# Up projection of a GeGLU block in seven half products for each pair of tiles, with the down projection behind it

## What is computed

```python
def conv_ffn(h, w_up, conv_w, conv_b, w_down, conv_state):
    u = jnp.einsum('btd,df->btf', h, w_up)             # 1024 -> 2 * 2816
    a, b = u[..., :D_FF], u[..., D_FF:]
    a_ext = jnp.concatenate([conv_state.astype(a.dtype), a], axis=1)
    conv = conv_b
    for j in range(CONV_W):                            # causal, width 3
        conv = conv + conv_w[j] * a_ext[:, j:j + T]
    out = jnp.einsum('btf,fd->btd', jax.nn.gelu(conv, approximate=True) * b, w_down)
```

## Time and profile before

| | us |
|---|---|
| median of 3 runs | 1754.72 |
| lowest and highest run | 1752.34, 1755.62 |
| span of the profiled execution (no other time of it is given) | 1750.5 |
| PE busy in that span | 1720.8 |

### The profile page before, as it was taken

How to read it: one execution, slowest core, us unless ns; L and a number is a source line. 1 busy time by engine, 2 the same in 40 slices (tenths; PEclk the granted TensorE clock), 3 DMA queues, 4 the chain that set the end, 5 groups by cost and what they waited for, 6 DMA issues and landing times.

```text
span 1750.5 us, 27949 instructions
## 1 busy us (share of the span) xinstructions
PE 1720.8 (98%) x11791; PEld 1640.1 (94%) x11791; DVE 749.9 (43%) x1027; ACT 494.6 (28%) x816; POOL 160.3 (9%) x232
## 2 busy tenths in 40 slices
PE   7999999999999999999999999999999999999998
PEld 6999889888888899999978999999999999999997
DVE  6421244444530255565544453433424434434345
ACT  5211244434443244331233321121121211211212
POOL 5100000000010024300033300000000000000001
PEclk9999999999999999999999999999999999999999
DMA  9774433231247686343441211102111111021004
GB/s 358 233 224 152 151 103 117 89 126 54 90 144 227 158 251 157 88 145 133 162 140 67 94 49 49 49 25 65 48 34 49 49 49 49 25 72 47 27 13 192
DMA packets 161038, 190.33 MB, mean 109 GB/s; under 512 B 14306, under 2 KB 139506, under 8 KB 160921
## 3 DMA queue, kind: packets, MB, share of 16 engines
q1 hardware_dynamic: 140488, 171.17, 30.3%
q10 hardware_dynamic: 19424, 17.21, 3.1%
q0 software_dynamic: 1008, 0.23, 0.1%
HBM read 146.70 MB, written 41.87 MB: 108 GB/s over the span
## 4 chain that ended last, share of the span: by engine, by line
PE 68%; ACT 1%; DVE 1%; issue 1%; POOL 0%; DVEq 0%; ACTq 0%; POOLq 0%
PE ps L162 46%; PE ps L1455 10%; PE ps L2655 4%; PE ps L2730 1%; PE ps L3230 1%; PE ps L3201 1%; PE ps L1811 0%; PE ps L2264 0%; PE ps L2222 0%; PE ps L2256 0%; PE ps L2625 0%; PE ps L2712 0%; POOL h_a L2441 0%; PE ps L2258 0%; PE ps L1821 0%
## 5 line engine op out<-in xcount | busy, mean ns | idle before, releaser
L162 PE MATMUL ps<-mg_hi,w_hi 128*128 128x352 f32 x1008 | 218.0, 324 | 0.3 <-issue 0.3
L162 PE MATMUL ps<-mg_hi,w_lo 128*128 128x352 f32 x1008 | 217.3, 323 | 0.0
L162 PE MATMUL ps<-mg_lo,w_hi 128*128 128x352 f32 x1008 | 217.0, 323 | 0.0
L162 PEld LDWEIGHTS ps<-mg_hi,w_lo 128*128 128x128 f32 x1008 | 173.1, 188 | 0.0
L162 PEld LDWEIGHTS ps<-mg_hi,w_hi 128*128 128x128 f32 x1008 | 171.6, 189 | 0.5 <-issue 0.5
L162 PEld LDWEIGHTS ps<-mg_lo,w_hi 128*128 128x128 f32 x1008 | 171.2, 188 | 0.0
L3056 DVE TENSOR_TENSOR f_t<-f_t,ps 128x1056 f32<-128x1056 f32 x80 | 100.3, 1253 | 151.2 <-PE ps L162 151.2
L147 DVE TENSOR_TENSOR w_lo<-w_raw,w_hi 128x2048 fp32r<-128x2048 f32 x59 | 136.7, 2317 | 56.8 <-ACT w_hi L143 56.8
L143 ACT ACTIVATE w_hi<-w_raw 128x2048 fp32r<-128x2048 f32 x59 | 112.9, 1914 | 124.6 <-PE ps L162 120.0
L1332 PE MATMUL ps<-acts_hi,w_hi 128*128 128x352 f32 x384 | 132.8, 346 | 2.9 <-ACT out_z L1164 2.3
L1455 PE MATMUL ps<-acts_hi,w_hi 128*128 128x352 f32 x384 | 128.0, 333 | 3.9 <-PEq L1073 2.3
(11 more groups left out here) (452 smaller groups left out, 3034.7 us busy)
## 6 DMA issues: line engine op xcount, KB each, us to landing
w_raw<-in_w_up SPq DMA_DIRECT2D x22, 1024.0 KB, 5.1
w_raw<-in_w_in SPq DMA_DIRECT2D x21, 1024.0 KB, 5.8
w_ada_chunks<-in_w_ada ACTq DMA_DIRECT2D x32, 512.0 KB, 7.4
w_raw<-in_w_down SPq DMA_DIRECT2D x11, 1024.0 KB, 4.8
z_scratch<-out_z SPq DMA_DIRECT2D x48, 176.0 KB, 1.8
z_scratch<-gate_ev SPq DMA_DIRECT2D x48, 176.0 KB, 4.7
w_ada_chunks<-in_w_ada SPq DMA_DIRECT2D x16, 512.0 KB, 8.3
chunks<-z_scratch SPq DMA_DIRECT2D x24, 256.0 KB, 4.4
```

Source lines behind the costliest of these rows:

```text
L162: mm = pe.matmul(ps[:, bank + b, 0:TB], w[wi][:, k, j * P:(j + 1) * P], (a_hi, a_lo)[ai][:, k, b * TB:(b + 1) * TB], start=(n == 0), stop= ...
```

## The change

**Units.** The up projection goes in units of one chunk (two output tiles), 22 in all; even units are a chunks, odd ones b chunks. Unit 0 stays an ordinary product (in four banks of 264 columns instead of three of 352). Units 1 to 21 take Strassen's scheme: the two output tiles, the two halves of the inner size (4 x 128 each) and the two halves of the tokens (528 each) form 2 x 2 blocks, and seven half products replace eight. A half product is 4 inner tiles x 3 passes x 2 banks = 24 matmuls of 264 columns.

**Sums in front.** Four sums of token blocks (T1 to T4, 128 x 2112 numbers each) are made once, between unit 0 and unit 1, by DVE and POOL, and split. For every unit POOL makes four sums of weight blocks (128 x 512), and all seven weight pieces of 512 columns are split by ACT and DVE one at a time, each as soon as its product of the unit before has ended.

**Sums behind.** The seven products accumulate in three pairs of banks; ACT copies intermediate sums out, DVE adds three of them from PSUM for each unit.

**Order.** The down projection no longer alternates with the up projection: all units come first. The rows g of ten pairs go to DRAM (`g_store`) and come back (`g_load`) for ten down pairs afterwards; the last pair stays on chip. The first down pair copies into `f_t`, so its clearing falls away. Token columns are reordered into four groups of 256 prompt tokens and 8 sample tokens, which splits some copies of the mixer in two.

```diff
+def half_product(u, r, bank, columns, first):
+    w = [piece(x, r) for x in (whi_all, wlo_all)]
+    order = products(HK)
+    pe.wait_ge(wp_lo, product(u, r))
+    for n, (k, wi, ai) in enumerate(order):
+        for q in range(2):
+            mm = pe.matmul(ps[:, bank + q, 0:QW], w[wi][:, k, :], columns(ai, k, q), ...)
+    mm.then_inc(u_prod, 1)
...
+def unit(u):                                   # on PE
+    half_product(u, A11, xb, of_h2(0, 0), True)
+    if u > 1: pe.wait_ge(y_added, ops_until(u - 1))
+    half_product(u, A12, YB, of_h2(HK, 0), True)
+    pe.wait_ge(x_copied, p1_copied(u))
+    if u == 1: pe.wait_ge(t_lo_s, 1)
+    half_product(u, PS2, xb, of_t(T2_), False)
+    ...                                        # u == 1: t_lo_s 2, else v_added
+    half_product(u, PS1, VB, of_t(T1_), True)
+    pe.wait_ge(x_copied, 2 * ops_until(u))     # u == 1: t_lo_s 3 too
+    half_product(u, PS3, xb, of_t(T3_), False)
+    pe.wait_ge(v_copied, ops_until(u))
+    half_product(u, PS4, VB, of_h2(HK, 2), False)
+    pe.wait_ge(x_added, ops_until(u))          # u == 1: t_lo_s 4 too
+    half_product(u, A22, xb, of_t(T4_), False)
...
+def weight_sums(u):                            # on POOL, for every unit
+    ...                                        # waits for the load, and from u = 3 for piece PS4 of unit u - 1
+    pool.tensor_tensor(at_(PS1), weight_part(u, PS1), weight_part(u, A22), ALU.add)
+    pool.tensor_tensor(at_(PS2), at_(PS1), weight_part(u, A11), ALU.subtract)
+    pool.tensor_tensor(at_(PS3), weight_part(u, A11), weight_part(u, PS1), ALU.subtract)
+    pool.tensor_tensor(at_(PS4), weight_part(u, A12), at_(PS2), ALU.subtract)
...
+pool.wait_ge(h_lo, NTT)                        # start of the part, POOL
+pool.tensor_tensor(r22[:], b22(mg_hi), b22(mg_lo), ALU.add)
+weight_sums(1)
+pool.tensor_tensor(t_raw[T3_][:], r22[:], r12[:], ALU.subtract)
...                                            # then clears, state copies, weight_sums(2)
+dve.wait_ge(h_lo, NTT)                         # start of the part, DVE
+dve.tensor_tensor(r12[:], b12(mg_hi), b12(mg_lo), ALU.add)
+dve.tensor_tensor(t_raw[T1_][:], r12[:], b11(mg_hi), ALU.subtract)
+dve.tensor_tensor(t_raw[T1_][:], t_raw[T1_][:], b11(mg_lo), ALU.subtract)
+dve.wait_ge(t_pool, 1)
+dve.tensor_tensor(t_raw[T2_][:], r22[:], t_raw[T1_][:], ALU.subtract)
+dve.tensor_tensor(t_raw[T4_][:], b21(mg_hi), t_raw[T2_][:], ALU.subtract)
+t_low(T2_, 2)
+piece_lo(dve, 1, PS2)
+t_low(T1_, 2)
+piece_lo(dve, 1, PS1)
+y_add(1)
+dve.tensor_tensor(t_raw[T4_][:], t_raw[T4_][:], b21(mg_lo), ALU.add)
+piece_lo(dve, 1, PS3)
+t_low(T3_, 3)
+piece_lo(dve, 1, PS4)
+piece_lo(dve, 1, A22)
+x_add(1)
+t_low(T4_, 4)
...                                            # pieces of unit 2, v_add(1), convolutions 0 and 1, b times g
+for u in range(2, UNITS_UP):                   # on DVE
+    piece_lo(A11 of u + 1); y_add(u); piece_lo(A12, PS2); x_add(u)
+    piece_lo(PS1, PS3); v_add(u); piece_lo(PS4)
+    # a units: convolve(u), piece_lo(A22), convolve(u + 1); b units: three products with g, piece_lo(A22)
...
-for k in range(KT):
-    pool.memset(f_t[:, k, :], 0.0).then_inc(f_add, 1)
...
+for i in range(DOWN_PAIRS):                    # on PE, behind the units and the 44 transposes
+    pe.wait_ge(w_lo_ready, FFN0 + 2 + i)
+    pe.wait_ge(g_lo_s, i + 1)
+    for k in range(KT):
+        ...                                    # k 0: y_added, v_added; k 1: lv_rows; else the add two tiles back
+        gemm_tile(pe, i % 2, 2, D_MODEL, k, g_hi[i % 2], g_lo[i % 2], 2 if k % 2 == 0 else 5)
+pe.wait_ge(f_add, KT * DOWN_PAIRS - 1)
+pe.wait_ge(f_samples, 1)
 rows_so_far(0)
```

More of the change, by code:

```diff
@@ L2770, in build, with x_bank, is_a @@
[L2770 to L2773, removed]
+    f_add, f_samples = sem("f_add"), sem("f_samples")
+    MADE_R12, MADE_T1_HALF, MADE_T1, MADE_T2, MADE_T4_HALF, MADE_T4 = range(1, 7)
+    A11, A12, PS2, PS1, PS3, PS4, A22 = range(PRODUCTS)
+    SUM_PIECES = (PS1, PS2, PS3, PS4)
+    T2_, T1_, T3_, T4_ = range(4)
+    YB, VB = 2, 4
+    def x_bank(u):
+        return 0 if u % 2 else 6
+    def is_a(u):
+        return u % 2 == 0
@@ new lines, in _ @@
+                    piece_hi(act, 1, PS2)
+                    piece_hi(act, 1, PS1)
+                    for u in range(1, UNITS_UP):
+                        more = u + 1 < UNITS_UP
+                        p1_copy(u)
+                        if u == 1:
+                            for r in (PS3, PS4, A22):
+                                piece_hi(act, u, r)
+                            t_up(T3_, t_pool, 2)
+                        if u == 2:
+                            gelu(1)
+                        if more:
+                            piece_hi(act, u + 1, A11)
+                            piece_hi(act, u + 1, A12)
+                        if not is_a(u) and u > 1:
+                            gelu(u - 1)
+                        u_copy(u)
+                        if more:
+                            piece_hi(act, u + 1, PS2)
+                        p5_copy(u)
+                        if u == 1:
+                            t_up(T4_, t_made, MADE_T4)
+                        if more:
+                            piece_hi(act, u + 1, PS1)
+                        if not is_a(u) and u > 1:
+                            gelu(u)
+                        if more:
+                            piece_hi(act, u + 1, PS3)
+                            piece_hi(act, u + 1, PS4)
+                        else:
+                            g_up(0)
+                            down_hi(0)
+                            g_up(1)
+                        if is_a(u):
+                            x_take(u)
+                        if more:
+                            piece_hi(act, u + 1, A22)
+                        if u == 1:
+                            gelu(0)
@@ L3087, in _, with convolve @@
[L3087 to L3091 removed]
+                    def convolve(f):
+                        for w in range(CONV_W):
+                            conv_op(f, w)
@@ new lines, in _ @@
+                    t_low(T1_, 2)
+                    piece_lo(dve, 1, PS1)
+                    y_add(1)
+                    dve.tensor_tensor(t_raw[T4_][:], t_raw[T4_][:], b21(mg_lo), ALU.add).then_inc(t_made, 1)
+                    piece_lo(dve, 1, PS3)
[3 more added lines that the diff above has]
+                    x_add(1)
+                    dve.wait_ge(t_made, MADE_T4)
+                    t_low(T4_, 4)
+                    for r in (A11, A12, PS2, PS1):
+                        piece_lo(dve, 2, r)
@@ L3181, in _ @@
+                    for u in range(1, UNITS_UP):
+                        unit(u)
                     pe.wait_ge(a_kept, 2 * FT)
+                    pe.wait_ge(xa_taken, UNITS_UP - 2)
                     for c in range(LV_F):
```

750 lines of the change are left out of this document (506 added, 244 removed).

## The result

The changed kernel takes **1724.37 us** (median of 4 runs, 1723.48 to 1724.97) beside 1754.86 for the kernel before (4 runs): a ratio of 0.983, 95% interval 0.981 to 0.984, 30.5 us less. Forecast were 1732.5 us, range 1708 to 1744, faster by over 0.2%. The direction and the range held; the point was 8 us too high. The profiled execution has a span of 1722.8, 27.7 less than that of before, and a time of 1724.58.

The account below looks back on a forecast made before the run. PE, busy in 98% of the span, bounds the kernel through matmul time and any wait. Terms -55.0 + 0.5 + 24.9 + 2 + 3.6 + 1.8 = -22.2 take the span from 1750.5 to 1728.3; plus 4.2: 1732.5 us, range 1708 to 1744.

Parts of the forecast that it names:

- products, 21 units: Up projection, units 1 to 21: 168 matmuls of 264 columns at 123 ns, 20.66 us a unit, saving 55.0 us (48 to 62).
- unit 0: Ordinary first unit: 192 narrower matmuls and a later last token tile make PE end 0.5 us later (0 to +2).
- start of unit 1, with slow matmuls: Units 1 and 2: PE waits 24.9 us for half sums of alternating DVE and POOL, plus 2 for slow matmuls.
- up to down: Between up and down projection: first tile waits 0.45 us, third 3.1 for DVE's first add; +3.6 (0 to 6).
- down loop: Down projection: keeps its 1440 matmuls, DVE's work fits, the fifth-tile add comes just in time; 0 (to +2).
- last add and sample copy: Behind the down projection: last add (1.25) and sample copy (0.4), formerly under up products, lie bare; +1.8 us (1 to 3).
- The start is covered: Rival at unit 1's start: DVE and POOL overlap or POOL finds gaps, PE waits 3.9 instead of 24.9; 1709.5 us, chance 0.15.
- DVE and POOL bound every unit: Rival for the up units: POOL's sums at 3.3 us each add 4.6 us a unit; 1825 us, chance 0.05.
- the point of no gain: Step of the slower rival: at 2.4 us per POOL sum, late `x_add` costs 1.1 us a unit and eats the gain.
- The end: Waits before the first down tiles, about 4 us, and before the token rows, about 2 us.
- From span to time: Whole kernel: forecast span 1728.3 plus 4.2, the earlier runs' median above the profiled span, gives 1732.5 us.

Follow-up runs that it names:

- the 5.15 above: Changed kernel with the second down pair's low halves made behind the first adds: 32 transposes took 5.15 us instead of 3.84; median 1722.6 us, ratio 0.981 to 0.984.

## Why the prediction came out 8 us too high

Point by point, in us of span; "measured" is from PE's timelines of before and after, and the terms add to -28.1 where the spans differ by 27.7.

| term | forecast | measured |
|---|---|---|
| products, 21 units | -55.0 | -59.2 (168 x 121.8 ns = 20.46 against 23.28) |
| unit 0 | +0.5 | +0.7 (959.52 to 984.71; before 957.41 to 981.91) |
| start of unit 1, with slow matmuls | +26.9 | +22.8 (452.5 less 3528 x 121.8 ns) |
| up to down | +3.6 | +3.1 (0.56 and 2.51) |
| down loop | 0 | +0.5 (235.8 less the 2.51, against 1440 x 161.7 ns) |
| last add and sample copy | +1.8 | +1.9 |
| ahead of unit 0 | 0 | +2.1 |

**What bounds the kernel, the places, the mechanism: right.** The gain comes from the matmuls left out, the loss from one chain of DVE and POOL in turns, and units 3 to 21 wait for nothing. *The start is covered* fell as a forecast of this order of work (two long queues do alternate). That its 1709.5 lies by the 1709.0 of the kernel with unit 1 plain is luck: it was counted down from a forecast 8 us too high, and that kernel makes 2.9 us more matmuls. *DVE and POOL bound every unit* fell too, by the width that the runs with more sums show. Its step "the point of no gain" was mis-sized, since it let the turns make `x_add` late. DVE's adds from PSUM in b units, `x_add` among them, have the same records with four sums a unit (after, 1060 to 1430) and with twelve (1060 to 1480):

```profile
L3319 DVE TENSOR_TENSOR b_sums<-b_sums,ps 128x528 f32<-128x528 f32 x28 | 19.6, 701 | 28.4 <-PE ps L3542 28.4
```

```profile
L3322 DVE TENSOR_TENSOR b_sums<-b_sums,ps 128x528 f32<-128x528 f32 x27 | 18.8, 696 | 20.1 <-PE ps L3545 20.1
```

Other DVE work, with both operands in SBUF, did get longer: the convolution's second and third step from a mean of 1.75 us to 2.26.

**Products: mis-sized by 4.2 us.** The step between the earlier trace rows was interpolated to 122.4 ns, and 0.6 added because the loop of the earlier trace rows steps slower than the earlier trace rows. The narrow matmuls take 121.8, so half of the error is the addition and half the interpolation. By the formula of the Trainium skill (TensorE: Matmul & The Clock Gate, section Back-to-back issue gap), which the page gives for the isolated gap of a warm matmul, an estimated 112.5 ns would come out for this width; the trace lies 9 ns above it, as it did by 10 to 12 for the two widths before.

**Start: mis-sized by 4.1 us.** Up to PS3's first matmul PE had lost 19.4 us (1015.82 - 984.71, less 96 x 0.1218) where 14.6 + 1.4 + 6.1 = 22.1 were forecast: a turn of DVE and POOL is 3.36 long and was walked with 3.6, since each instruction got a whole record of its own from the earlier trace rows, and T3 took 4.5 for 4.7. The slow matmuls of PS2 were swallowed by the wait behind, as forecast, and those of PS3 cost 21 x 98 ns = 2.1 for 2. Behind them 2.8 were forecast in A22 and unit 2, thin waits that hang on the same walk, and at most 1.3 came.

**The end, right.** Both waits are where they were put, behind the same instructions, and go when those are moved.

**From span to time: it held, for a reason that was not known.** 4.2 us were added, the distance of before's median from the profiled span. The time of each profiled run lies 1.8 above its span, so the other 2.4 are a difference between runs. Windows of before and after, in code that the change left alone:

```profile
500.00:510.00 10.00, 7.67 (x53) 7.42 (x52) 1.35 (x5) 4.64 (x6) 4.02 (x3) 1.00 0.67 148
```

```profile
500.00:510.00 10.00, 7.67 (x43) 7.33 (x42) 1.65 (x6) 3.18 (x6) 4.02 (x3) 0.83 0.62 137
```

The profiled run of before had full clock there (mean 0.999 over the run); all traces of the changed kernels had not, and some 1.6 of the 2.1 us ahead of unit 0 are lost there, the time of the ten matmuls that this window has less. Many other runs of before show a mean of 0.998 and spans of 1752.1 to 1752.9, about what such a stretch would make of them. So these 2.1 us probably come from the run and not from the change; it is not shown, since only one run of before was traced. Then the spans differ by 30, as the medians do, and the products and the start, 8.3 us, are the whole error.

## What to carry to other kernels

When an algorithm saves matmuls at the price of sums, look first at the one place where the sums have no matmuls beside them, and cover it with one unit of the plain product rather than shorten it: 2.9 us bought back 20.6 here. Two engines that take turns are one queue: move work to the faster of the two even if it is the busy one (4.3 us here), and expect an instruction taken out of the chain to be replaced by those behind it in the other queue, as the sums of unit 2 were. If an engine names a lightly loaded engine as its releaser, ask what that one's queue was waiting for.

## What the runs showed of the hardware that was not expected

**A wait costs more than its length.** Windows of after, behind the waits before PS2 and PS3, with the stretch between them:

```profile
1003.50:1006.80 3.30, 3.30 (x15) 3.30 (x16) 3.30 (x2) 0.06 (x1) 3.26 (x1) 0.50 0.00 0
1007.00:1010.80 3.80, 3.80 (x33) 3.80 (x33) 3.80 (x4) 1.13 (x2) 3.80 (x2) 1.00 0.02 4
1015.90:1020.50 4.60, 4.60 (x21) 4.60 (x22) 1.02 (x2) 0.00 (x0) 1.20 (x3) 0.50 0.53 167
```

After 12.7 and 4.7 us without work the granted clock was 0.50, 1.2 GHz, and matmuls stepped by 3.30 / 15 = 220 ns instead of 122: some 3.5 us on 36 of them, of which the 1.5 in PS2 were hidden by the next wait. Even behind 1.86 us without work it was 0.50 in some runs (the 5.15 above) and full in others, so a short wait costs its length in one run and nearly twice that in another, which may be a part of the spread of 2 us between runs; one run of each kernel was traced, so that is not shown.

**Turns are by whole instruction.** POOL's sums, 1.16 us from the end of the DVE instruction ahead, were recorded with 3.28 to 3.41 us, and DVE's instructions, 2.21, with 3.31 to 3.34, in each of four turns in a row. The Trainium skill (SBUF — State Buffer, section Who interferes with whom) says that the first to issue keeps the shared ports to its end; the trace agrees, and shows besides that with both queues full the two took strict turns, so that each moved on by one instruction in 3.36 us.
